# One Silu activation on ScalarE in place of Tanh on ScalarE and a product on VectorE, after a causal convolution

## What is computed

```python
def _causal_conv_silu(x, w):
    kw = w.shape[0]
    s = x.shape[1]
    xp = jnp.pad(x, ((0, 0), (kw - 1, 0), (0, 0)))
    y = sum(w[j].astype(jnp.float32) * xp[:, j:j + s] for j in range(kw))
    return jax.nn.silu(y)

# in the layer
qkv = _causal_conv_silu(dn_qkv, dn_conv_w)       # 256 tokens x 6144 channels
dq, dk_, dv_ = jnp.split(qkv, 3, axis=-1)
dq = _l2norm(_heads(dq, DN_HEADS))
dk_ = _l2norm(_heads(dk_, DN_HEADS))
dv_ = _heads(dv_, DN_HEADS)
```

## Time and profile before

| | |
|---|---|
| timed runs | 1913.24, 1913.38, 1915.33 us; median 1913.38 |
| span of the profiled execution | 1913.3 us |
| TensorE (PE) busy | 1895.3 us |
| VectorE (DVE) busy | 1398.8 us |
| ScalarE (ACT) busy | 947.8 us |
| GpSimd (POOL) busy | 344.2 us |
| convolutions and their scores | about 43 to 400 us |

### The profile page before, as it was taken

One profiled execution on the slowest core, in us unless ns is written; L12 is line 12 of the kernel. 1 busy time (PEld: TensorE's weight loads), 2 busy tenths in 40 slices (PEclk: granted clock), 3 DMA queues, 4 the chain that ended last, 5 costly groups with the idle time before them and its releaser, 6 DMA issues.

```text
span 1913.3 us, 27611 instructions
## 1 busy us (share of the span) xinstructions
PE 1895.3 (99%) x10948; PEld 1638.9 (86%) x10948; DVE 1398.8 (73%) x1970; ACT 947.8 (50%) x1409; POOL 344.2 (18%) x543
## 2 busy tenths in 40 slices
PE   8999999999999999999999999999999999999998
PEld 8989999878888999988888888888888888888886
DVE  5686777676989888989989768665465686657675
ACT  6556566654544333444445465554444455544544
POOL 1025344351122222223223200000000000111000
PEclk9999999999999999999999999999999999999999
DMA  7455454555788877777888857755556543544563
GB/s 257 133 167 176 122 172 137 155 160 172 262 274 286 271 257 239 238 261 241 298 284 300 305 200 231 230 181 184 191 173 209 176 131 123 182 151 149 181 229 132
DMA packets 209744, 393.16 MB, mean 205 GB/s; under 512 B 13000, under 2 KB 62448, under 8 KB 208208
## 3 DMA queue, kind: packets, MB, share of 16 engines
q1 hardware_dynamic: 191248, 323.17, 51.6%
q0 software_dynamic: 18224, 68.17, 11.3%
q10 hardware_dynamic: 144, 0.07, 0.0%
HBM read 387.13 MB, written 4.23 MB: 205 GB/s over the span
## 4 chain that ended last, share of the span: by engine, by line
PE 94%; DVE 2%; ACT 2%; issue 1%; DMA 0%; SPq 0%; DVEq 0%; ACTq 0%
PE GB L2152 53%; PE GB L2179 18%; PE GB L2164 9%; PE GB L2167 5%; PE SB L415 1%; PE SB L1723 1%; PE SB L1715 1%; PE SB L819 1%; PE SB L784 1%; PE SB L1822 1%; PE SB L1829 1%; PE SB L1179 1%; ACT WH L2071 1%; DVE WL L2076 0%; DMA xin<-in_x 0%
## 5 line engine op out<-in xcount | busy, mean ns | idle before, releaser
L2076 DVE TENSOR_TENSOR WL<-raw,WH 128x1024 fp32r<-128x1024 f32 x605 | 732.3, 1237 | 197.4 <-ACT WH L2071 196.4
L2071 ACT ACTIVATE WH<-raw 128x1024 fp32r<-128x1024 f32 x605 | 621.7, 1057 | 320.5 <-PE GB L2152 227.1
L2152 PE MATMUL GB<-WH,uHL 128*128 128x512 f32 x1792 | 484.9, 392 | 0.0
L2152 PEld LDWEIGHTS GB<-WH,uHL 128*128 128x128 f32 x1792 | 333.3, 188 | 68.1 <-issue 0.5
L2179 PE MATMUL GB<-uHL,WH 128*128 128x256 f32 x2048 | 294.9, 287 | 1.6 <-DVE uHL L451 1.6
L2152 PE MATMUL GB<-WH,hHL 128*128 128x512 f32 x1024 | 279.5, 395 | 0.0
L2152 PE MATMUL GB<-WL,uHL 128*128 128x512 f32 x896 | 276.0, 389 | 0.0
L2179 PEld LDWEIGHTS GB<-uHL,WH 128*128 128x128 f32 x2048 | 265.6, 192 | 6.2 <-issue 3.4
L2152 PEld LDWEIGHTS GB<-WH,hHL 128*128 128x128 f32 x1024 | 190.6, 188 | 41.1 <-issue 2.7
L1409 DVE SCALAR_TENSOR_TENSOR macc<-wm,csil,macc 128x512 f32<-128x512 f32 x300 | 209.3, 745 | 2.8 <-DMA wm<-in_w_mod 1.7
L2152 PEld LDWEIGHTS GB<-WL,uHL 128*128 128x128 f32 x896 | 168.2, 188 | 35.4
(11 more groups left out here) (403 smaller groups left out, 1968.3 us busy)
## 6 DMA issues: line engine op xcount, KB each, us to landing
raw<-in_w_in SPq DMA_DIRECT2D x512, 512.0 KB, 4.6
raw<-in_w_out SPq DMA_DIRECT2D x96, 512.0 KB, 5.0
wm<-in_w_mod POOLq DMA_DIRECT2D x64, 512.0 KB, 5.5
wm<-in_w_mod POOLq DMA_DIRECT2D x64, 256.0 KB, 4.2
xin<-in_x SPq DMA_DIRECT2D x4, 512.0 KB, 5.7
E<-decay_rows POOLq DMA_DIRECT2D x4, 512.0 KB, 4.2
hres<-in_x POOLq DMA_DIRECT2D x1, 2048.0 KB, 10.8
cin<-in_ctx POOLq DMA_DIRECT2D x1, 2048.0 KB, 11.3
```

What stands on the lines that cost most here:

```text
L2071: e.activation(place(s)[0][:, :, :], raw[s % NR][:, :, :], ACT.Copy).then_inc(*wh.inc("WH", s))
L2076: e.tensor_tensor(low[:, :, :], raw[s % NR][:, :, :], f32(high[:, :, :]), sub).then_inc(*wl.inc("WL", s))
L2152: m = e.matmul(banks[j][:, :], x[:, c, 128 * j:128 * j + 128], w[:, k, :], start=i == 0 and k == 0 and n == 0, stop=i == 7 and k == 1 and ...
```

## The change

ScalarE takes Silu of `y` and writes it straight to `qk` or `vv`. VectorE's product, the tile `th` and the halving of the taps go. The waits for `qk` or `vv` being free again move from VectorE to ScalarE, and who waited for VectorE's product waits for ScalarE's activation.

```diff
         def conv_act(e, r):
...
             e.wait_ge(*slot.at("mm", end("qkv", r)))
-            if r == 0:
-                e.wait_ge(*init.at("taps"))
-            else:
-                e.wait_ge(*cv_dve.at("dst", r - 1))
+            if r:
+                e.wait_ge(*cv_act.at("t", r - 1))
...
             e.wait_ge(*cv_dve.at("33", r))
-            e.activation(th, y, ACT.Tanh).then_inc(*cv_act.inc("t", r))
+            if n and kind < 2:
+                e.wait_ge(*qp_dve.at("p3", n - 1))
+            elif n:
+                e.wait_ge(*qv_pe.at("t1", n - 1))
+            e.activation(taken(kind, n), y, ACT.Silu).then_inc(*cv_act.inc("t", r))
...
-                e.wait_ge(*cv_dve.at("dst", r))
+                e.wait_ge(*cv_act.at("t", r))
...
         def conv_dve(e, r):
...
-            e.wait_ge(*cv_act.at("t", r))
-            if n and kind < 2:
-                e.wait_ge(*qp_dve.at("p3", n - 1))
-            elif n:
-                e.wait_ge(*qv_pe.at("t1", n - 1))
-            e.scalar_tensor_tensor(out=taken(kind, n), in0=th, scalar=1.0, in1=y, op0=add,
-                                   op1=mul).then_inc(*cv_dve.inc("dst", r))
             yield
...
         def values_pe(e, bank, n):
-            e.wait_ge(*cv_dve.at("dst", 3 * n + 2))
+            e.wait_ge(*cv_act.at("t", 3 * n + 2))
...
-                if s == 0:
-                    e.tensor_scalar(vcol[:, CONV:VCOLS], vcol[:, CONV:VCOLS], 0.5, None, mul).then_inc(*init.inc("taps"))
```

More of the change, by code:

```diff
@@ L385, in hybrid_program @@
         stored = [sem(f"stored{n}") for n in range(4)]
-        init = steps("init", "ones", "eps", "taps")
+        init = steps("init", "ones", "eps")
         nx_act = steps("nx_act", "warm", "s0", "s1", "s2", "s3", "sqrt", "x1a", "x1b", "x1c")
@@ L696, in hybrid_program @@
         cv_act = steps("cv_act", "y", "t")
-        cv_dve = steps("cv_dve", *[f"{j}{sh}" for j in range(4) for sh in (1, 2, 3)], "dst")
+        cv_dve = steps("cv_dve", *[f"{j}{sh}" for j in range(4) for sh in (1, 2, 3)])
         l2_pe, l2_act, l2_pool = steps("l2_pe", "s"), steps("l2_act", "sq", "ln0", "ln1", "ex"), steps("l2_pool", "n")
@@ L717, in conv_act @@
             banks = GB[2 * (r % 2):2 * (r % 2) + 2]
-            y, th = yth[:, 0], yth[:, 1]
+            y = yth[:, 0]
             e.wait_ge(*slot.at("mm", end("qkv", r)))
-            if r == 0:
-                e.wait_ge(*init.at("taps"))
-            else:
-                e.wait_ge(*cv_dve.at("dst", r - 1))
+            if r:
+                e.wait_ge(*cv_act.at("t", r - 1))
             for j in range(4):
@@ L1101, in dnz_act @@
             else:
-                e.wait_ge(*cv_dve.at("dst", 11))
+                e.wait_ge(*cv_act.at("t", 11))
             for i in range(2):
```

## The result

| | before | after |
|---|---|---|
| median of the timed runs | 1914.04 us (1913.24 to 1915.33, 4 runs) | 1921.88 us (1921.65 to 1923.01, 4 runs) |
| ratio | | 1.0042, 95% interval 1.0027 to 1.0056 |
| span of the profiled execution | 1913.3 us | 1921.2 us |

The changed kernel is 0.42% slower. The forecast was 1918.9 us in a range of 1915.4 to 1921.8: the sign was right, the size too small, and the measured time is 0.1 us beyond the range.

A forecast was written before the change was run, and what follows sets the result against it. TensorE, busy 1895.3 of 1913.3 us, was taken to bound the kernel, so only its waits count. Added table loads cost 2.48 + 3.12 = 5.6 us, giving 1918.9 us, range 1915.4 to 1921.8.

The forecast's parts named there:

- The removed product is worth nothing: VectorE's twelve products L771, 14.5 us, lie where VectorE waits for ScalarE anyway or behind; no gain on the path.
- Rival (b): A switch to or from Silu costs the drain as well, 2.8 us; sum 16.7, 1930 us; chance 0.03.
- (c): Silu is served by Exp's table, so no loads are added and all four waits stay: 1913.3 us; chance 0.07.
- (d): VectorE's freed time, or loads slipping into waits, leave 2 to 3.5 us of the sum: 1916 us; chance 0.12.
- (e): Faster: no loads, and VectorE's free time ends all four waits, at most 2.9 us, 1910.4 us; chance 0.02.
- Place one: Unit r = 2, at 117 us: loads lengthen TensorE's wait for the decayed scores from 1.47 to 3.95 us, +2.48.
- U2's delay of 0.97: Units r = 5, 8 and 11: late Silu delays WL, so U2, which TensorE already waits for, comes 0.97 us late.
- the second delay of 0.07: Units r = 5, 8 and 11: the second load delays TensorE's second pair of scores by 0.07 us more, bounds 0 and 0.4.
- the 0.4 us left at r = 1: WL at 94.05, though later, still ends 0.4 us before TensorE's slot, so costs nothing; bounds 0 and 0.3.
- Rival (a): TensorE's clock falls in the 3.95 us wait near 126 us, costing 1.75 us more: 1920.7 us; chance 0.14.
- Places two to four: Units r = 5, 8 and 11, at 204, 293 and 381 us: loads cost +1.04 us each, 3.12 in all.
- All of them hang on ScalarE: Claim that all four TensorE waits, at L819 and L946, depend on ScalarE, so VectorE's free time would hardly end them.

The follow-up runs named there:

- the last one above: Order with ScalarE's activation later, five start matmuls, and U2 and the copy ahead of WL (n = 0, 1, 2): 1909.97 us with Silu, 1911.32 us with Tanh and product.
- the two kernels with a part of the Silu: Changed kernel with Silu only for some units, Tanh for the rest: r = 0, 1, 2, 1918.90 us; r = 5, 8 and 11, 1918.15 us.
- the late Silu: Changed kernel with ScalarE's Silu two slots later, behind the high parts of two weights and the decay's Exp: 1913.49 us, ratio 0.9994.
- the late Tanh: Kernel before with ScalarE's Tanh and VectorE's product two and one slots later, behind a weight's high part and the decay's Exp: 1913.96 us, ratio 1.0002.

## Why the prediction was right or wrong

**Right.** *The removed product is worth nothing*: Tanh in Silu's place gives the time of before. That holds in this order of work; in the last one above it is worth more than the loads cost. *Silu behaves as Ln does*: 17 loads of 1283 ns, 12 at Silu, 4 at the decay's Exp, one at L532, and that of r = 3 ended in its wait. *The price of a load, 1.31 us from end to start*: 115.92 to 117.24 gives 1.32. Rival (b) with its drain had nothing for it; rivals (c), (d) and (e) fell as well. *Place one's wait of 3.95 us, U2's delay of 0.97, the second delay of 0.07, the 0.4 us left at r = 1*: measured 3.95, 0.98, 0.08 (so far as the chain has it, see below) and no wait. *Losses at four places and nowhere else*: the ledger, and the two kernels with a part of the Silu.

**Wrong, the step that failed.** The clock. Rival (a) had the right mechanism and place, and I gave it 0.14 and left it out of the sum. The reason against it, that this pause comes out of dense work, was no row's; the only row on a long pause spoke for it, and a pause made 2.7 times as long as the one the trace has there (1.47 us) should have been treated as unknown, with both ends in the range. Its price was too small also: 1.75 us was taken from a fall that lasted 3.5 us, from 16 to 19.5, and the one here lasted 7. (For that shorter fall it was even too much: without it, these 24 matmuls take 3.13 us and not 2.88, so it cost 1.50.) What the runs showed in place of the overlooked term: the clock fell in the wait of 3.95 us and cost 2.64 us, and with the wait filled by 12 matmuls it stayed up and the 2.64 were gone. With it the sum is 2.48 + 2.64 + 3.12 = 8.2.

**The terms mis-sized.** Places two to four: 1.30 for 1.04, 0.26 short each. I read TensorE's own arrival at the second scores from a piece of the chain, 215.71, where its order of time has 215.54: a wait there also costs the 0.17 us of overlap with the matmuls ahead, and the step took 0.07 more behind it. I took what TensorE stands still as a wait's whole price.

**The base.** I set the span, 1913.3, against the median of 1913.38 as the same. They agree by chance. A timed execution is 1.8 to 2.0 us longer than its span: after, 1923.01 against 1921.2, before, 1915.33 against 1913.3. The profiled execution of before was one with the clock's fall at the start, worth 1.5, and that of 1913.38 wasn't, by its time. With a fourth execution (1914.70) the median of before became 1914.04, between its two groups: 0.66 of the 2.98 us between the forecast and the measured time are this. The ledger without the start is 5.12 + 3.91 = 9.0 us, and the medians differ by 7.8. Some 0.7 of that gap is the median between the groups; that not every fall at place one lasts as long as the profiled one is the likely rest, but was not shown. That the miss of the range is only 0.1 us is luck of the same kind: the losses of the profiled execution are 3.4 us over the sum.

**Wrong, without harm here.** "All of them hang on ScalarE": at L946 they hung on GpSimd's product. The row had both (WL idle until WH, then 1.67 us long), and I used the length for the delay's size and not for its cause. Had I carried it on, the late Silu's expectation would have been 1912 and not 1911.

## To carry to other kernels

A load of a function table costs what is queued behind it: the same 1283 ns were worth nothing in most slots, and two of them close together cost 1.3 us at each of three places where TensorE already waited, and 5.1 us at the one where they made a wait of 3.95 us in which TensorE's clock fell. Before exchanging a function, list for each call what is loaded ahead of it and what stands behind it on ScalarE, and move the call behind the work that others wait for. And price a lengthened wait of TensorE in two parts, the wait and what a fall of the clock would add, unless a row shows as long a wait without one.

## What the runs showed of the hardware beyond what was expected

- TensorE's clock fell in all three profiles in which it stood still for 3.95 us out of dense work (the changed kernel, Silu with the product, Silu for r < 3). It stayed low for 7, 3.3 and 6.8 us, at a cost of 2.6, 1.4 and 2.5 us. It stayed at 1.00 behind the 1.47 us of the kernel before. The same fall near the start, behind two pauses of 1.0 and 1.6 us around eight short transposes, comes in some executions only. 12 small matmuls in the pause of 3.95 us kept the clock at 1.00, and so did five in the one of 1.6 us near the start, in the profile and, by their times, in all ten executions.
- The Trainium skill (ScalarE: Activation LUTs, What ACT_TABLE_LOAD costs) has 1283 ns for a load, which every load of the traces agrees with, and about 1380 ns of drain, which none shows: where ScalarE didn't wait for anything else, 1.30 to 1.37 us lie between the end of one activation and the start of the next, with 1.31 or 1.32 as a rule.
- VectorE's subtraction of two operands in SBUF made next to no headway while GpSimd's product of two SBUF operands ran (2.60 us in place of 1.23, and 1.01 us from the product's end to the next instruction, whenever it had started), but VectorE's product with an operand in PSUM ran beside it in its usual 0.69 us.
- It goes the other way too, as far as two rows can show: in the late Tanh, one of GpSimd's small products (TB, 128x30) took 1.10 us at 403.15, while WLs ran without a gap on VectorE, and one of 128x28 took 0.23 us at 408.07, while VectorE stood idle.
